# Hybrid attention, short convolution and MoE block: sort steps moved inside a gate block, half of the shared gate and up moved into the first expert pass, another order of the ring of weights, and the split of the rows shared among three engines

## The reference

```python
def moe_ffn(h, p):
    xf = h.reshape(-1, shp[-1])
    idx, w = route(xf, p["w_router"], p["router_bias"])   # sigmoid, 2 of 4 groups, 4 of 32 experts
    comb = jnp.sum(jax.nn.one_hot(idx, N_EXPERTS) * w[..., None], axis=1)
    g = jnp.einsum("td,edf->tef", xf, p["w_exp_gate"])    # 32 experts, d 2048, f 256
    u = jnp.einsum("td,edf->tef", xf, p["w_exp_up"])
    a = jax.nn.silu(g) * u * comb[..., None]
    routed = jnp.einsum("tef,efd->td", a, p["w_exp_down"])
    shared = (jax.nn.silu(xf @ p["w_sh_gate"]) * (xf @ p["w_sh_up"])) @ p["w_sh_down"]  # f 512
    return (routed + shared).reshape(shp)
```

## Time and profile before

| | us |
|---|---|
| median of three runs | 1166.63 (1166.46 to 1171.25) |
| profiled execution, its own time | 1170.56 |
| its span | 1168.80 |
| TensorE busy in the span | 1029.9 |
| VectorE busy | 559.9 |
| ScalarE busy | 224.3 |
| GpSimd busy | 9.1 |
| mean rate of the transfers over the span | 325 GB/s |

### The profile page before, as it was taken

One profiled execution on the slowest core, in us unless ns is written; L12 is line 12 of the kernel. 1 busy time (PEld: TensorE's weight loads), 2 busy tenths in 40 slices (PEclk: granted clock), 3 DMA queues, 4 the chain that ended last, 5 costly groups with the idle time before them and its releaser, 6 DMA issues.

```text
span 1168.8 us, 15738 instructions
## 1 busy us (share of the span) xinstructions
PE 1029.9 (88%) x6017; PEld 574.8 (49%) x6031; DVE 559.9 (48%) x1114; ACT 224.3 (19%) x455; POOL 9.1 (1%) x13
## 2 busy tenths in 40 slices
PE   1879999999999998999799997999779988998973
PEld 0525568888875455444488542434234333334421
DVE  1301167855814683985445261465255343446414
ACT  4301110000002354000230131122022112213203
POOL 0000000000000000000000000000000000000002
PEclk9889999999999999999899998999999998999996
DMA  8998979999845726999507799999999999999992
GB/s 335 354 368 316 340 244 357 367 346 329 276 162 188 256 96 235 335 387 343 216 1 289 306 409 408 409 406 408 409 408 409 394 410 409 409 383 405 409 401 87
DMA packets 156343, 380.30 MB, mean 325 GB/s; under 512 B 12322, under 2 KB 43888, under 8 KB 154096
## 3 DMA queue, kind: packets, MB, share of 16 engines
q1 hardware_dynamic: 156272, 379.35, 86.5%
HBM read 377.22 MB, written 2.10 MB: 325 GB/s over the span
## 4 chain that ended last, share of the span: by engine, by line
PE 67%; DMA 13%; DVE 8%; SPq 6%; ACT 3%; issue 2%; ACTq 0%; POOL 0%; DVEq 0%
PE ps L570 65%; DMA ring<-in_w_exp_down 10%; SPq L486 4%; DMA ring<-in_w_mod 4%; DVE xres L1816 3%; DVE nreg L1777 1%; ACT nreg L1072 1%; DVE part L1806 1%; DVE nreg L1810 1%; SPq L374 1%; SPq L366 1%; DVE tiny L1552 0%; PE ps L640 0%; ACT ring L1226 0%; PE ps L815 0%
## 5 line engine op out<-in xcount | busy, mean ns | idle before, releaser
L570 PE MATMUL ps<-nreg,ring 128*128 128x256 f32 (+1 forms) x1280 | 302.5, 397 | 8.3 <-ACT nreg L1072 5.9
L570 PEld LDWEIGHTS ps<-nreg,ring 128*128 128x128 f32 x1280 | 244.9, 193 | 62.1 <-issue 19.5
L570 PE MATMUL ps<-ring,nreg 128*32 128x512 f32 (+1 forms) x1344 | 173.8, 608 | 19.0 <-DMA ring<-in_w_exp_up 19.0
L1404 DVE SCALAR_TENSOR_TENSOR part<-ring,csT,part 128x512 f32<-128x512 f32 x232 | 174.4, 752 | 8.9
L570 PEld LDWEIGHTS ps<-ring,nreg 128*32 128x32 f32 (+1 forms) x1344 | 51.1, 116 | 132.2 <-issue 132.2
L570 PE MATMUL ps<-ring,conv 128*32 128x512 f32 (+1 forms) x672 | 95.7, 656 | 18.4 <-DMA ring<-in_w_exp_down 18.4
L570 PE MATMUL ps<-ring 128*128 128x512 f32 x256 | 110.8, 592 | 0.0
L570 PE MATMUL ps<-nreg,conv 128*128 128x512 bf16 x251 | 65.4, 385 | 34.3 <-DVE xres L1816 29.5
L570 PEld LDWEIGHTS ps<-ring 128*128 128x128 f32 x256 | 48.6, 190 | 60.4 <-issue 60.3
L1816 DVE TENSOR_TENSOR xres<-xres,ps 128x512 f32<-128x512 f32 x96 | 61.6, 684 | 22.9 <-PE ps L570 22.9
L570 PE MATMUL ps<-pick,qnT 128*128 128x128 bf16 x384 | 66.9, 220 | 0.4 <-ACT nreg L1258 0.4
(11 more groups left out here) (224 smaller groups left out, 917.2 us busy)
## 6 DMA issues: line engine op xcount, KB each, us to landing
ring<-in_w_mod SPq DMA_DIRECT2D x88, 1024.0 KB, 9.5
ring<-in_w_exp_gate SPq DMA_DIRECT2D x128, 512.0 KB, 13.1
ring<-in_w_exp_up SPq DMA_DIRECT2D x128, 512.0 KB, 15.4
ring<-in_w_exp_down SPq DMA_DIRECT2D x128, 512.0 KB, 13.8
ring<-in_w_in SPq DMA_DIRECT2D x15, 2048.0 KB, 12.3
ring<-in_w_out SPq DMA_DIRECT2D x8, 2048.0 KB, 10.8
ring<-in_w_mod SPq DMA_DIRECT2D x4, 2048.0 KB, 19.8
ring<-in_w_sh_gate SPq DMA_DIRECT2D x2, 2048.0 KB, 9.4
```

Of the source, the lines that this page charges most:

```text
L570: return nc.tensor.matmul(o, l, r, start=start, stop=stop)
L1404: ins = V.scalar_tensor_tensor(out=out_, in0=w_, scalar=scale, in1=acc_, op0=ALU.mult, op1=ALU.add)
```

## The change

The sort's transpose and matmul stand after 8 and after 10 k of the second gate block. The shared weights are loaded by column halves: gate and up blocks 0 and 1 are computed before pass 0, blocks 2 and 3 inside pass 0, one ahead of q = 3 and three after the gather ahead. The shared down products stand in passes 1, 4, 7 and 9. The units take their places from a list: 0 to 7 in slots 5, 1, 3 and 2, 8 to 15 in the same again, 16 to 19 in slots 5 and 1, 20 to 23 in slots 4 and 0, then the twelve in turn. GpSimd does the first subtraction of the split, ScalarE the cast, VectorE the second subtraction. xg moves from nreg[:, 0:2048], where hT is still in use, to nreg[:, 5120:7168]. The lines left out do the same for the unit numbers of the other loads, the views of w_sh_gate and w_sh_up, and the passes for experts with more tokens than their room.

```diff
           ("T", 7))
-DOWN = {0: 0, 3: 1, 6: 2, 9: 3}
-BASES = [sum(6 * EXPERTS[kind] + (j in DOWN) for j, (kind, _) in enumerate(PASSES[:t])) for t in range(len(PASSES))]
+DOWN = {1: 0, 4: 1, 7: 2, 9: 3}
+BASES = [sum(6 * EXPERTS[kind] + (j in DOWN) for j, (kind, _) in enumerate(PASSES[:t])) for t in range(len(PASSES) + 1)]
+PLACE = [2 * s + h for s in (0, 1, 2, 3, 0, 1, 2, 3, 0, 1, 4, 5) for h in range(2)]
+PLACE += [(j + 4) % UNITS for j in range(24, BASES[-1])]
+TURN = [PLACE[:j].count(PLACE[j]) for j in range(len(PLACE))]
+BEFORE = [max(i for i in range(j) if PLACE[i] == PLACE[j]) if TURN[j] else None for j in range(len(PLACE))]
 OVER = ((1, 0, 96, 2), (14, 1, 64, 2), (16, 15, 32, 1))
+OVER_UNIT = BASES[-1] - 6
 M_ANY, M_OVER, NMORE = 0, 1, NE
...
-        RING = (5, 1, 2, 3, 4, 0)
+        RING = (5, 1, 3, 2, 4, 0)
         def unit(n):
-            n %= UNITS
-            return slot[RING[n // 2]][:, 2048 * (n % 2):2048 * (n % 2) + 2048]
+            at = PLACE[n]
+            return slot[RING[at // 2]][:, 2048 * (at % 2):2048 * (at % 2) + 2048]
...
         ygate = nreg[:, 4096:5120].rearrange("p (b n) -> p b n", b=2)
-        gainB = nreg[:, 5120:7168]
+        gainB = nreg[:, 0:2048]
         junk = conv[:, 512:1536].rearrange("p (b n) -> p b n", b=2)
         shT = [buf[:, T * k:T * k + T] for buf in (krT, krs) for k in range(2)]
         shS = conv[:, 512:1536].rearrange("p (k t) -> p k t", k=4)
-        gained = nreg[:, 0:2048]
-        xg = nreg[:, 0:2048].rearrange("p (c s) -> p c s", c=KC)
+        gained = nreg[:, 5120:7168]
+        xg = nreg[:, 5120:7168].rearrange("p (c s) -> p c s", c=KC)
         yes = nreg[:, 2048:4096].bitcast(BF16)
...
-        SH_UP = ((1, 10), (2, 11), (4, 1), (0, 11))
+        SH_UP = ((1, 10), (4, 1), (2, 11), (0, 11))
...
                 s = SH_UP[i][0]
-                sp.dma_start(slot[s].rearrange("p (q x) -> p q x", q=2), src[:, 2 * half:2 * half + 2, :])\
-                  .then_inc(w_full[s], 16)
+                for q in range(4):
+                    sp.dma_start(slot[s][:, 1024 * q:1024 * q + 1024].rearrange("p (j n) -> p j n", j=4),
+                                 src[:, q, :, 256 * half:256 * half + 256]).then_inc(w_full[s], 16)
             sp.wait_ge(wo_full, 3)
             load_shared_up(0, sg, 0)
             sp.wait_ge(wo_half, 4)
+            load_shared_up(2, su, 0)
+            sp.wait_ge(acc_done, 16 * 16)
             load_shared_up(1, sg, 1)
-            sp.wait_ge(acc_done, 16 * 16)
-            load_shared_up(2, su, 0)
             sp.wait_ge(wo_full, 4)
...
                     sp.dma_start(unit(n)[:, 1024 * g:1024 * g + 1024],
-                                 src[:, bass.ds(e, 1), q, :].rearrange("p a x -> p (a x)")).then_inc(unit_in[n % UNITS], 16)
+                                 src[:, bass.ds(e, 1), q, :].rearrange("p a x -> p (a x)")).then_inc(unit_in[PLACE[n]], 16)
...
-            def first_room(n):
-                if n == 2:
+                                 sd[:, 2 * c:2 * c + 2, 512 * m:512 * m + 512]).then_inc(unit_in[PLACE[n]], 16)
+            def first_room(s):
+                if s == 1:
+                    sp.wait_ge(sh_gate, 2)
+                elif s == 3:
+                    sp.wait_ge(hT_full, 8)
+                    sp.wait_ge(split_ready, 4)
+                elif s == 2:
+                    sp.wait_ge(sh_up, 2)
+                elif s == 4:
                     sp.wait_ge(sh_gate, 4)
-                elif n == 6:
-                    sp.wait_ge(hT_full, 8)
-                    sp.wait_ge(split_ready, 2)
-                elif n == 8:
+                elif s == 0:
                     sp.wait_ge(sh_up, 4)
             def room(n):
-                if n < UNITS:
-                    first_room(n)
+                if not TURN[n]:
+                    first_room(RING[PLACE[n] // 2])
                 else:
-                    sp.wait_ge(unit_used, n - (UNITS - 1))
+                    sp.wait_ge(unit_used, BEFORE[n] + 1)
...
+            for t in range(2):
+                pool.wait_ge(split_act, t + 1)
+                nc.gpsimd.tensor_tensor(xh[:, t, :], xh[:, t, :], parts[0][:, t, :], ALU.subtract).then_inc(split_ready, 1)
...
-            def shared_up(i, m):
-                base, full = (2, sh_up) if i else (0, sh_gate)
-                if m >= 2:
-                    pe.wait_ge(sh_act if i else sh_silu, m - 1)
-                for half in range(2):
-                    s, use = SH_UP[2 * i + half]
-                    if m == 0:
-                        pe.wait_ge(w_full[s], 16 * use)
-                    for k in range(8):
-                        ins = mm(ps[:, base + m % 2, T * (m // 2):T * (m // 2) + T], k_of(s, 8)[:, k, 128 * m:128 * m + 128],
-                                 hT[:, 8 * half + k, :], half == 0 and k == 0, half == 1 and k == 7)
-                ins.then_inc(full, 1)
+            def shared_up(i, m, ks=range(KC)):
+                s, use = SH_UP[2 * i + m // 2]
+                if ks[0] == 0:
+                    if m % 2 == 0:
+                        pe.wait_ge(w_full[s], 16 * (use + 3))
+                    if m >= 2 and i:
+                        pe.wait_ge(sh_silu, m + 1)
+                bank = ps[:, 2 * i + m, 0:T] if m < 2 else ps[:, 2 + m, T * i:T * i + T]
+                for k in ks:
+                    ins = mm(bank, k_of(s, KC)[:, k, 128 * (m % 2):128 * (m % 2) + 128], hT[:, k, :], k == 0, k == KC - 1)
+                if ks[-1] == KC - 1:
+                    ins.then_inc(sh_up if i else sh_gate, 1)
...
             mm(ps[:, 5, 64:96], ones, mask[:, 1, :], False, True).then_inc(rank_full, 1)
-            shared_up(0, 1)
+            shared_up(0, 1, range(0, 8))
             pe.wait_ge(sort_in, 1)
             nc.tensor.transpose(ps[:, 6, 0:128], vrow[:, :], ident).then_inc(tbl_full, 1)
-            shared_up(0, 2)
+            shared_up(0, 1, range(8, 10))
             pe.wait_ge(tbl_out, 1)
             mm(ps[:, 7, 0:128], tblT, blocks, True, True)
             mm(ps[:, 7, 128:192], ones, sums, True, True).then_inc(sort_full, 1)
-            shared_up(0, 3)
-            for m in range(4):
-                shared_up(1, m)
-            pe.wait_ge(sh_silu, 4)
+            shared_up(0, 1, range(10, KC))
+            shared_up(1, 0)
+            pe.wait_ge(rank_ready, 1)
+            pe.wait_ge(sh_silu, 2)
             gather(0, (0, 1))
-            pe.wait_ge(rank_ready, 1)
+            shared_up(1, 1)
             gather(0, (2, 3))
-            pe.wait_ge(sh_act, 4)
+            pe.wait_ge(sh_act, 2)
             def wait_units(ns):
                 for n in ns:
-                    pe.wait_ge(unit_in[n % UNITS], 32 * (n // UNITS + 1))
+                    pe.wait_ge(unit_in[PLACE[n]], 32 * (TURN[n] + 1))
...
                         first += 1
+                    if base == 0 and q == 3:
+                        shared_up(0, 2)
                     if kind != "over":
...
                     gather(t + 1, (0,), last)
+                if base == 0:
+                    shared_up(0, 3)
+                    shared_up(1, 2)
+                    shared_up(1, 3)
                 pe.wait_ge(act_ready, t + 1)
...
                     pe.wait_ge(sh_gated, 2 * DOWN[t] + 2)
+                if base == 0:
+                    pe.wait_ge(sh_act, 4)
...
-            for n in range(4):
+            def shared_silu(n):
                 sc.wait_ge(sh_gate, n + 1)
-                nc.scalar.activation(shS[:, n, :], ps[:, n % 2, T * (n // 2):T * (n // 2) + T], ACT.Silu).then_inc(sh_silu, 1)
+                nc.scalar.activation(shS[:, n, :], ps[:, n if n < 2 else 2 + n, 0:T], ACT.Silu).then_inc(sh_silu, 1)
+            shared_silu(0)
+            for t in range(2):
+                sc.wait_ge(split_ready, t + 1)
+                copy(parts[1][:, t, :], xh[:, t, :]).then_inc(split_act, 1)
+            shared_silu(1)
...
-            def pair_pass(t, ahead=True):
+            def pair_pass(t, ahead=True, first=False):
                 sc.wait_ge(pickT_full, t + 1)
                 nc.scalar.activation(pickT, ps[:, 3, 0:256], ACT.Sign).then_inc(pickT_out, 1)
+                if first:
+                    shared_silu(2)
                 sc.wait_ge(gu_full, t + 1)
                 nc.scalar.activation(act[:, 0, :], ps[:, 2, 0:FF], ACT.Silu).then_inc(silu_done, 1)
+                if first:
+                    shared_silu(3)
+                    sc.wait_ge(sh_act, 3)
                 sc.wait_ge(actT_full, t + 1)
...
             for t in range(len(PASSES)):
-                pair_pass(t, ahead=t + 1 < len(PASSES))
+                pair_pass(t, ahead=t + 1 < len(PASSES), first=t == 0)
             for n in range(4):
...
                 ve.wait_ge(sh_silu, m + 1)
-                V.tensor_tensor(shT[m], ps[:, 2 + m % 2, T * (m // 2):T * (m // 2) + T], shS[:, m, :], ALU.mult)\
+                up = ps[:, 2 + m, 0:T] if m < 2 else ps[:, 2 + m, T:2 * T]
```

(25 more changed lines are left out.)

5 lines of the change are left out of this document (2 added, 3 removed).

## The result

| | kernel before | changed kernel |
|---|---|---|
| median of 7 runs each | 1169.07 us | 1175.74 us |
| lowest to highest | 1166.46 to 1171.26 | 1173.51 to 1179.52 |
| profiled execution (span) | 1170.56 (1168.80) | 1173.51 (1171.7) |

The ratio of the changed kernel to the one before is 1.0062, 95% interval 1.0043 to 1.0081: slower by 6.7 us between the medians. The forecast gave 0.53 to "same" (less than 0.5% from the kernel before) and 0.26 to "slower", so it put its weight on the wrong side of that bound; the time itself lies in the range. The 1166.63 from which the forecast started was the median of three runs of the kernel before; that of these seven is 2.4 us higher.

The account below looks back on a forecast made before the run. From 650 us the expert transfer stream sets the end, before that the TensorE, VectorE, TensorE chain producing the order. Terms -5.2 + 8.8 + 2.3 = +5.9 us on the 1166.63 median gave 1172.5 us, range 1160 to 1176.

Parts of the forecast that it names:

- how the numbers follow: Step turning cases into chances, with 0.5% (5.8 us) as bound: faster 0.21, same 0.53, slower 0.26.
- (a): Likeliest case: both GpSimd subtractions hold up VectorE's selection chain; 1172.5 us, own range 1168 to 1176, chance 0.50.
- (b): Rival: GpSimd and VectorE do not exclude each other here, or small operations pass; 1161 us, chance 0.32.
- (c): Rival: only one GpSimd subtraction meets the selection chain; no change, 1166.6 us, chance 0.13.
- half clock: TensorE, after idling for mask_ready, works at 1.2 GHz for a while: 2.3 us, bounds 0 and 3.4.
- Selection chain, 8.8 us late: VectorE's small operations before mask_ready wait for GpSimd's two subtractions: 8.8 us late, bounds 3.8 to 9.4.
- Stream 5.2 us earlier: The unbroken expert transfer stream starts 5.2 us earlier, at unit 29: 699.0 instead of 704.2.
- Part 1: Sort steps inside the second gate block: order of the experts at 603.7 instead of 613.13, 9.4 us earlier by itself.
- Part 2: Half of gate and up inside pass 0: pass 0 27.7 us earlier, first expert matmul 625.7; 1 KB rows cost nothing.
- Part 3: Ring of expert buffers: unit 28 waits for pass 1's q = 0; some 7 us hole, head start mostly lost.
- (d): Rival: room for unit 28 is there in time and the stream keeps its head start; -13 us, 1154, chance 0.05.
- Part 4: Row split on three engines: GpSimd's subtractions, 4.8 us each, exclude VectorE's two-operand steps from 592.1 to about 602.

Follow-up runs that it names:

- e1: Changed kernel with the split of the rows put back on VectorE alone, GpSimd idle; 1171.21 us, ratio to the kernel before 1.0022.
- e8: Kernel before with only the sort's transpose after 8 k and its matmul after 10 k of the second gate block; 1169.09 us, ratio 1.0000.
- e2: Changed kernel with GpSimd's subtractions held until the sort inputs and both up blocks ahead of the first gather; 1164.77 us, ratio to before 0.9964.
- e3: Changed kernel with one placement line different, so units 28 to 31 replace 16 to 19, not 20 to 23; 1168.57 us, ratio to before 0.9987.
- e5: Kernel before with two GpSimd subtractions of 128x2048 added, results unused; 1180.83 us, ratio 1.0116.
- e7: Kernel before with two GpSimd copies of 128x2048 added, results unused; 1174.69 us, ratio 1.0059.
- e6: Kernel before with two GpSimd memsets of 128x2048 added; 1175.65 us, ratio 1.0060.
- e4: Changed kernel with the edits of e2 and e3 together; 1158.96 us, ratio to the kernel before 0.9898.
- e11: Changed kernel with the second gate block before the mask wait, sort steps in the first up block, both up blocks before the gather; 1172.26 us, ratio to before 1.0029.
- e12: e11 with the unit placement of e3 and GpSimd's subtractions held until mask_ready; 1163.59 us, ratio to the kernel before 0.9953.

## Why the prediction was right or wrong

**What failed: how the numbers follow.** The sum was +5.9 us, on the bound of 0.5% itself, and the step there split case (a) in halves, same and slower, and then gave the rivals (b) and (c), in which nothing or little is held up, 0.45. The ground of (b), the larger with 0.32, was that VectorE's operations are short and may pass; that of (c), that only one subtraction meets the chain. The rows show the opposite of both: two operations of 0.17 us are held, 3.80 and 3.98 us, one by each subtraction. Even with all the chance on (a), "slower" would only have been level with "same": the sum itself was also short, by 0.8 us (6.7 measured), and its terms erred in both directions. The one that was too small by most is the half clock, 2.3 for 3.43:

- **Selection chain, 8.8 us late: measured 7.44**, inside the bounds 3.8 to 9.4. GpSimd's operation took 4.05 us instead of 4.8, 1.5 us less for two. The victims were named wrongly: not the two-operand steps at 592.84 and 593.10 but the two TENSOR_SCALARs with one SBUF operand ahead of them. The forecast had looked only for operations with two operands; that the price came out near it is luck in this point, since one operation a subtraction is held either way.
- **Half clock, 2.3 us: measured 3.43**, the upper bound. It was sized from a stretch in which TensorE had 4.6 us of work at half clock; here it worked from 604.47 until the clock was back near 611, some 7 us.
- **Stream 5.2 us earlier: about 4.4.** Unit 29 would flow at 699.0 + 7.44 + 3.43 = 709.9 by the forecast's own count; it did near 710.7. Of the 0.8 us between these two, 0.66 are the wait of q = 2, 1.96 instead of 1.3.

-4.4 + 7.44 + 3.43 = +6.5, against 6.7 between the medians. The remaining 2.4 us between 1172.5 and 1175.74 are in the starting point, 1166.63 from three runs against 1169.07 from seven.

**Part 1** was right: 603.7 was forecast for an undisturbed order, 604.35 (e1) and 603.38 (e8) were measured. **Part 2** was right: 625.7 for the first expert matmul by itself, 627.01 in e2, and 636.11 in the changed kernel, where 625.7 + 10.9 = 636.6. The 1 KB rows had no visible cost in any wait for w_sh_gate or w_sh_up on the way. **Part 3** was right, and with it the arithmetic that speaks against (d): the hole stands at 700 to 707, and e3, without it, is 7.6 us faster. **Part 4** was right in its mechanism and place, shown by e5 alone and by e1 and e2 from the other side.

**The rivals.** (b), no exclusion, and (c), one meeting, are excluded by two rows of 3.80 and 3.98 us. (d) is excluded by the issue at 704.98. The marks that were set for the forecast stood: VectorE rows of 4 us at 592 and 596 (on 8 columns, though), mask_ready at 604.2 to 604.4 (near 606 was said), the order at 614.12, the clock's dip at 600 to 613, and 17 GB/s at 700 to 705. The dips near 920, given 0 to 1 us, were absent from the profiled executions of the changed kernel and of those built on it, and present in those of e5 to e7, which are built on the kernel before (slices of 387 to 390 GB/s where the earlier trace rows has 394); but the medians show no gain by it, and what makes them is open. The spread of 5 us between executions of one kernel is explained in part: behind the last wait for down weights (2.4 to 3.1 us) the same 32 matmuls took 3.64 us in e7 and e8, where the granted clock stayed at 1.00, 5.34 in the kernel before, the changed one and e2, and 6.34 in e6, where it fell to 0.50.

**Where the gain went, then.** By themselves, the first two parts move pass 0 forward by 27 us (e2) and the order by 9.75 (e8). The two subtractions cost 10.9 us of the time and the order of the ring 7.6; without both (e4) the change is worth 10.6 us. Whether the holes that e4 keeps (ahead of units 22 and 30) can be closed was not tried.

## What to carry to other kernels

Before a long GpSimd operation is given to an idle engine, look at which VectorE instructions stand in the same microseconds and what hangs on them: the price is not GpSimd's time but how late the chain behind VectorE is, plus the half clock of whatever engine idles for it, here 7.4 + 3.4 us for 8.1 us of work; a wait that moved it 10 us later (e2) took it off the path to the order. Count a ring of buffers by when each new unit's predecessor is done, not by its depth: one line of placement was worth 7.6 us. And measure a part of a change in the kernel in which it is to stand: the earlier order was worth nothing in one (e8) and 6 us or more in the other (e11 against e2).

## What the runs showed of the hardware that was not expected

- A VectorE TENSOR_SCALAR on 128x8 fp32 with one SBUF operand is held as long as GpSimd's instruction lasts: 3.80 and 3.98 us for 0.17. A SCALAR_TENSOR_TENSOR on 31 columns took 4.10 (e2). A TENSOR_REDUCE that began at 591.86, 0.08 us into the subtraction, kept its 0.19 (none ran later in a GpSimd operation), and so did the reads of PSUM in e2 (0.18 and 0.19).
- A GpSimd memset, which reads nothing, holds such an instruction too: 1.51 and 1.76 us.
- Two subtractions of GpSimd took 8.09 to 8.14 us whichever VectorE instructions they held (8.10 in e2, 8.14 in e12); no run has them undisturbed. One VectorE instruction gets through between two operations of GpSimd and the next is held again, so the number of GpSimd operations sets the number of victims.
- For 128x2048 fp32, GpSimd took 4.05 us to subtract, 1.89 to copy, 1.80 to set; VectorE took 2.29 to subtract.
- 8.4 us of idle TensorE were followed by half clock for some 7 us of work, at a cost of 3.3 to 3.4 us; an idle time of 3.93 (e6) cost about 1.7 on the matmuls after it.
